# Moving the split of w_out's pooling half behind the state evacuations at the end of the first stage

## The reference

```python
h = modulate(rmsnorm(x, norm1_g), sh1, sc1)      # sh1, sc1 ... from silu(c) @ w_ada + b_ada
u = h @ w_in                                     # (tokens, 1024)
pool_out = pool_mixer(u[..., :512], ...)         # trailing means 2/4/8/16, a 128x128 map per group
ssm_out  = ssm_mixer(u[..., 512:], ...)          # 32 groups of 16 channels, 64 complex states each
mix = concatenate([pool_out, ssm_out], -1) @ w_out
x = x + g1 * mix
x = x + g2 * hier_moe(modulate(rmsnorm(x, norm2_g), sh2, sc2), ...)
y = rmsnorm(x, final_norm_g)
```

## Time and profile before

| what | value |
|---|---|
| median of three runs | 1162.4 us |
| the profiled execution's own time | 1166.91 us |
| its span | 1165.1 us |
| PE busy | 1075.8 us (92%) |
| DVE busy | 765.8 us (66%) |
| ACT busy | 516.1 us (44%) |
| POOL busy | 312.9 us (27%) |
| mean granted clock of TensorE | 0.974 |

### The profile page before, as it was taken

One profiled execution on the slowest core, in us unless ns is written; L12 is line 12 of the kernel. 1 busy time (PEld: TensorE's weight loads), 2 busy tenths in 40 slices (PEclk: granted clock), 3 DMA queues, 4 the chain that ended last, 5 costly groups with the idle time before them and its releaser, 6 DMA issues. The chain is left out here.

```text
span 1165.1 us, 18015 instructions
## 1 busy us (share of the span) xinstructions
PE 1075.8 (92%) x5413; PEld 806.9 (69%) x5414; DVE 765.8 (66%) x1256; ACT 516.1 (44%) x732; POOL 312.9 (27%) x370
## 2 busy tenths in 40 slices
PE   3799999999797989999999989999999999999992
PEld 2357777776465668787787646888888788888860
DVE  5557475747579954378887788555777555555375
ACT  5134252422333225446665243544566455544373
POOL 0046272626141000030000003333334433333244
PEclk9799999999989999999999999999999999999996
DMA  9933656567774459386766557897799877775597
GB/s 281 316 109 101 190 158 198 154 180 246 222 156 162 137 160 250 148 226 215 248 222 217 163 217 253 238 294 216 216 272 271 219 212 220 222 208 113 111 358 306
DMA packets 165460, 244.75 MB, mean 210 GB/s; under 512 B 65327, under 2 KB 122831, under 8 KB 161255
## 3 DMA queue, kind: packets, MB, share of 16 engines
q1 hardware_dynamic: 135065, 167.54, 45.0%
q0 software_dynamic: 17040, 57.87, 19.0%
q10 hardware_dynamic: 13302, 18.66, 4.6%
HBM read 169.36 MB, written 75.84 MB: 210 GB/s over the span
## 5 line engine op out<-in xcount | busy, mean ns | idle before, releaser
L126 PE MATMUL experts_psGU<-weights_we_hi,experts_x_hi 128*128 (+1 forms) x344 | 141.2, 410 | 2.1 <-DVE experts_x_lo L2714 1.0
L128 PE MATMUL experts_psGU<-weights_we_lo,experts_x_hi 128*128 (+1 forms) x344 | 136.0, 395 | 0.0
L127 PE MATMUL experts_psGU<-weights_we_hi,experts_x_lo 128*128 (+1 forms) x344 | 136.0, 395 | 0.0
L2540 POOL DMA_INDIRECT acc_d<-experts_o_sb,experts_to_col x40 | 71.0, 1776 | 209.2 <-DMA acc_d<-experts_o_sb,experts_to_col 109.5
L126 PE MATMUL front_psM<-front_hT_hi,front_w_hi 128*128 128x512 f32 x256 | 106.7, 417 | 0.9 <-DVE front_hT_lo L1043 0.9
L127 PE MATMUL front_psM<-front_hT_hi,front_w_lo 128*128 128x512 f32 x256 | 101.7, 397 | 0.0
L2733 DVE TENSOR_TENSOR experts_o_sb<-experts_psD,experts_g2r 128x1024 f32<-128x1024 f32 x43 | 52.7, 1225 | 74.5 <-PE experts_psD L128 74.5
L128 PE MATMUL front_psM<-front_hT_lo,front_w_hi 128*128 128x512 f32 x256 | 101.2, 395 | 0.0
L126 PEld LDWEIGHTS experts_psGU<-weights_we_hi,experts_x_hi 128*128 128x128 f32 x344 | 64.7, 188 | 20.9 <-issue 6.4
L128 PEld LDWEIGHTS experts_psGU<-weights_we_lo,experts_x_hi 128*128 128x128 f32 x344 | 64.6, 188 | 15.7
L2704 DVE TENSOR_TENSOR weights_we_lo<-weights_we_raw,weights_we_hi (+1 forms) x64 | 75.5, 1220 | 0.0
(11 more groups left out here) (530 smaller groups left out, 2522.3 us busy)
## 6 DMA issues: line engine op xcount, KB each, us to landing
front_raw<-in_w_ada SPq DMA_DIRECT2D x24, 1024.0 KB, 14.2
weights_we_raw<-in_exp_w_gate SPq DMA_DIRECT2D x16, 1024.0 KB
weights_we_raw<-in_exp_w_up SPq DMA_DIRECT2D x16, 1024.0 KB
weights_wd_raw<-in_exp_w_down SPq DMA_DIRECT2D x16, 1024.0 KB
front_xraw<-in_x_prompt SPq DMA_DIRECT2D x4, 2048.0 KB, 10.9
part_d<-middle_ev ACTq DMA_DIRECT2D x16, 512.0 KB, 3.8
middle_xt<-in_x_prompt SPq DMA_DIRECT2D x16, 512.0 KB, 4.8
middle_part<-part_d SPq DMA_DIRECT2D x16, 512.0 KB, 5.6
```

What stands on the lines that cost most here:

```text
L126: pe.matmul(out, l_hi, r_hi, start=start, stop=False)
L127: pe.matmul(out, l_lo, r_hi, start=False, stop=False)
L128: return pe.matmul(out, l_hi, r_lo, start=False, stop=stop)
L2540: pool.indirect_dma_start(acc_d, bass.IndirectOffsetOnAxis(tc[:, u, :], 0), osb[:, u, :], None, compute_op=ALU.add).then_inc(added, 16)
```

## The change

On ACT the four casts `out_hi` move from between the state evacuations to the end of its part of `front`. On DVE the four subtractions `out_lo`, and the wait for the stores of `u_d`, move to the end, behind the memsets. No instruction is added or removed, and the queues of SP, POOL and PE are as before.

```diff
@@ scalar @@
-                for i in range(4):
-                    state_inputs((3, 7, 9, 11)[i], (7, 9, 11, 12)[i])
-                    out_hi(i)
+                state_inputs(3, 12)
                 table(kk_fill(NCK - 1), P, 4)
                 for t in range(2):
                     state_inputs(12 + 2 * t, 14 + 2 * t)
                     act.wait_ge(T.m_in[t], 16)
                     act.copy(mp_hi[:, t], mraw[:, t]).then_inc(T.pmhi, 1)
+                for i in range(4):
+                    out_hi(i)
@@ vector @@
                 mod_row(ADA2_N - 1)
-                state_inputs(0, 8)
-                for u in range(2):
-                    dve.wait_ge(ust_out[u], 16 * STEP * 2 * NBLK)
-                out_lo(0)
-                state_inputs(8, 10)
-                out_lo(1)
-                state_inputs(10, 12)
+                state_inputs(0, 13)
                 kk_diag(NCK - 1)
-                state_inputs(12, 13)
-                out_lo(2)
-                state_inputs(13, 14)
-                out_lo(3)
-                state_inputs(14, PAIRS)
+                state_inputs(13, PAIRS)
                 dve.wait_ge(T.pmhi, 1)
                 tt(mp_lo[:, 0], mraw[:, 0], mp_hi[:, 0].bitcast(F32), ALU.subtract).then_inc(T.pmlo, 1)
                 dve.wait_ge(s["v_ev0"], PAIRS)
...
                 for i in range(2):
                     ins = dve.memset(H[:, i, :, NSEQ:NSEQ + 1], 0.0)
                 ch.link(ins)
+                for u in range(2):
+                    dve.wait_ge(ust_out[u], 16 * STEP * 2 * NBLK)
+                for i in range(4):
+                    out_lo(i)
```

## The result

The changed kernel is slower: 1168.4 us (median of 7 runs, 1165.76 to 1171.42) against 1162.83 us (7 runs, 1159.2 to 1165.6), ratio 1.0046 with a 95% interval of 1.0031 to 1.0061, that is +5.3 us (3.6 to 7.1). The forecast was +4.3 us.

The account below looks back on a forecast made before the run. The prediction took PE's waits for transfers, then DVE's release of the next stage, as the bound. A release 3.5 us later plus 0.8 us at the first product, on the 1162.4 median, gave 1166.7 us, range 1162.5 to 1169.3.

Parts of the forecast that it names:

- Step 1: PE before pair 12: runs on without the old stall, then waits 4.6 us for U's last load, until 318.3.
- ACT's table copy: ACT, before pair 12: its wait for an earlier table's store costs nothing, because the wait for U covers it.
- Step 2: PE, pairs 12 to 15: partly at half clock, last pair ends at 324.7, between bounds of 322.1 and 325.6.
- Step 3: Tail from PE's last pair to the release: 7.6 us against 2.6 us, so it grows by 5.0 us.
- the 0.91 us: End of the tail: time from DVE's last instruction to the release of the engines, taken as 0.91 us.
- 0.33, 0.62, 1.17, three of 1.13, 1.22: Tail in us: last state copy, second pooling cast, quarter 0's cast with DVE's start, subtraction spacings, last subtraction.
- Step 4: Release of the next stage: at 332.3 against 328.82, +3.5 us, with bounds of +0.9 and +4.4.
- Step 5: Next stage's first product: the slower clock after PE's longer stand adds +0.8 us, between nothing and 1.7 us.
- The sum: Whole kernel: +3.5 us at the release and +0.8 us at the first product give +4.3 us, 1166.7 us.
- Rival A: Before pair 12: U lands in time, PE runs through at full clock, -3.0 us, 1159.4 us; chance 0.10.
- Rival B: Pairs 12 to 15 mostly keep full clock, or the stage behind absorbs lateness: 1163.3 to 1164.7 us; chance 0.20.

Follow-up runs that it names:

- Experiment 2: Changed kernel, but POOL issues the two w_out transfers only when all loads of U have landed; ratio to the kernel before 0.9981.
- experiment 1: Changed kernel, but all eight moved instructions (ACT's casts, DVE's subtractions) stand between pair 11 and pair 12; ratio to the kernel before 0.9979.
- experiment 6: Changed kernel, but quarters 0 and 1 of the w_out split stand between pairs 11 and 12, quarters 2 and 3 behind the last pair; ratio to before 1.0001.
- Experiment 5: Changed kernel plus matmuls of no use on PE, 5 calls ahead of pair 12 and 7 behind the last pair; ratio to the kernel before 1.0001.
- experiment 3: Changed kernel, but U's last load has its own semaphore and doesn't wait for the load before it; ratio to the kernel before 0.9980.
- 7: Changed kernel with U's last load on its own semaphore and 7 calls of useless matmuls behind the last pair; ratio to the kernel before 0.9948.

## Why the prediction was right, point by point

**Step 1, how far PE gets: right.** PE ran to pair 12's turn (313.80 + 0.89 = 314.69) and waited for U until 318.6; the forecast was 318.3. The wait was 3.81, 4.46 and 4.76 us in the three profiles, against the 4.6 forecast. Experiment 2 shows the reason given, w_out's 2 MB: without them the same load lands in 2.8 us. ACT's table copy behind the store of the earlier table cost nothing, as said.

**Step 2, pairs 12 to 15: right in kind, 0.7 us too late.** Forecast 22.65 behind pair 0 (324.7 - 302.05); the three profiles gave 21.59, 22.22 and 22.01. The two lengths of the slow stretch were right, 3.4 and 6.6 us, and so was a value between; wrong was that it begins with pair 12. In the first and the third profile a stretch of 3.4 us began 1.2 and 0.6 us after pair 12 did, in the second the long one began 2.2 us before it, so that a third of it fell into the wait.

**Step 3, the tail: right in its sum of instructions, 0.7 us too long.** The term that failed is the 0.91 us from DVE's end to the release. Behind the four subtractions it is 331.08 - 330.79 = 0.29 us; 0.9 us stand there when the memsets are last, as in the kernel before and in experiment 1 (DVE idle 0.95 us before its next instruction, where after shows 0.34). The prediction took the 0.91 us for a fixed cost of the meeting. Everything else (0.33, 0.62, 1.17, three of 1.13, 1.22) is in the rows. That ACT and DVE had time for this work elsewhere is shown by experiment 1, and the price of 1.1 to 1.3 us a quarter by experiment 6.

**Step 4, the release: forecast +3.5 us, measured +2.0** (28.88, the mean of three, against 26.84, the mean of two); the two errors above, and both of one sign.

**Step 5, the first product: right.** DVE's wait is 2.45, 2.15 and 2.17 us after and 1.42 and 1.40 before, which is 0.85 us more in the mean, against the 0.8 forecast. Experiment 5 shows that it is the clock.

**The sum.** Forecast +4.3. The profiles show +2.9 at DVE's low part (39.53 against 36.63), and the timed runs +5.3 (3.6 to 7.1). So the forecast for the median lies between, and its mechanism was right, but that the number came so close is partly luck: the stretch that I argued about gave 1.4 us less than forecast, and by these runs at least 0.7 us of the measured difference is not in it. A part of that rest may be no cost at all. The 1162.83 us of before are the median of 7 runs; in the three later groups of runs, 79 in all, the median of before was 1165.6, 1164.45 and 1165.23, and the changed kernel's 1168.4 lies only 2.8 to 4.0 us above these. They come from other groups of runs, so this is a hint and not a measurement. The profiles show a candidate: a slow clock between 425 and 445, worth some 3 us, which one of two profiles of before and two of three of after had (157.8 and 157.5 us from DVE's low part to the output product, against 158.2 before). The third of after, with the full clock there, took 156.0 us, against 154.8 in the second of before; in it DVE waited a second time for its cast, 1.94 us at 355.00. Whether the change makes it likelier is open; these profiles don't tell.

**Rival A** (U in time) did not happen, but experiment 3 is that rival made by hand: forecast for it was a last pair at 15.3 behind pair 0 and -3.0 us; it gave 15.33 and 0.9980, -2.3 us (0.7 to 4.0). The rule of the Trainium skill that spoke for A (DMA: Bandwidth & Descriptors, Queues, rings and completion order) says that queues take turns by the packet. The traces don't show such turns where the load comes behind w_out, not at first: queue 0 had 99.5% of the engines from 310.8 to 313 before and 97.6% after, and U took 7.5 to 10.4 us in all ten profiles of that order. But the prediction also took more from the rule than it gives. In the earlier trace rows a packet of queue 0 holds 3.8 KB (0.81 MB in 211) and one of queue 1 0.26 KB (0.30 MB in 1168). If these packets are what takes turns, one each, U's 256 KB would be about half through when the 2 MB are done, by an estimate from these rows. So even turns need not have brought U in time; what helped was to have no w_out in the way (experiment 2, 2.8 us) or to come ahead of it (experiments 3 and 7, 5.2 and 6.2 us). **Rival B** (the stage behind takes up the lateness) is ruled out by experiments 1, 3 and 7, where a release 4.5 to 6.3 us earlier than in the changed kernel came out at the end, by the difference of the ratios, as 7.7 to 11.4 us, the clock's share behind the release included.

## What to carry to other kernels

When a wait is removed, ask what the engine meets next, and when that will be there: here the next operand was queued behind the very transfer whose wait was moved away, and the stall came back two pairs later. Work that waits for a slow transfer should go to the end only if there is no idle time between here and there; in the gap that the next wait leaves it was free, at the end it cost 1.1 to 1.3 us a piece. And a small load that the next step needs is to be issued before a large one that is needed later, where nothing on the path waits for the large one. An issue 0.6 us ahead was enough in two profiles and not in a third (5.2, 6.2 and 10.1 us); holding the large one back until the small one had landed gave 2.8 us, and cost its own wait at the end (experiment 2).

## What I had not expected of the hardware

An issue of the same 256 KB load 4 us earlier (307 instead of 311) turned 7.5 us to landing into 5.2 us (6.2 and 10.1 in two more profiles), while the 2 MB beside it took 9.6 us in the median of the two transfers, where the ten profiles of the usual order have 8.1 to 9.8. And the time from the last instruction of a stage to the next stage's start depends on which instruction is last: 0.9 us behind two memsets of 72 ns, 0.3 us behind a subtraction of 1.2 us. In the kernel the memsets are followed by a wait of DVE for its own semaphore, which stands ahead of the meeting only where they are last; that this wait is the difference is a guess that no run tests.
